# Attention weights scaled while they are turned: a product with a scaled diagonal in place of a scaled tile and a transpose

## The reference

```python
p_s = masked_softmax(einsum('btghd,btgnd->btghn', qg, ks), kpos <= q_pos)
o_s = einsum('btghn,btgnd->btghd', p_s, vs)
p_w = masked_softmax(einsum('btghd,blgd->btghl', qg, k_win), valid_w)
o_w = einsum('btghl,blgd->btghd', p_w, v_win)
out = g[..., 0:1] * o_c + g[..., 1:2] * o_s + g[..., 2:3] * o_w
```

## Time and profile before

| | us |
|---|---|
| median of three runs | 2237.94 (2236.41 to 2238.18) |
| profiled execution, its own time | 2232.05 |
| its span | 2230.2 |
| PE busy | 2080.6 (93%) |
| DVE busy | 760.7 (34%) |
| ACT busy | 470.9 (21%) |
| POOL busy | 406.0 (18%) |
| mean granted clock of TensorE | 0.956 |

### The profile page before, as it was taken

How to read it: one execution, slowest core, us unless ns; L and a number is a source line. 1 busy time by engine, 2 the same in 40 slices (tenths; PEclk the granted TensorE clock), 3 DMA queues, 4 the chain that set the end, 5 groups by cost and what they waited for, 6 DMA issues and landing times.

```text
span 2230.2 us, 28141 instructions
## 1 busy us (share of the span) xinstructions
PE 2080.6 (93%) x11199; PEld 1603.7 (72%) x11199; DVE 760.7 (34%) x1445; ACT 470.9 (21%) x869; POOL 406.0 (18%) x454
## 2 busy tenths in 40 slices
PE   4999999988878889999999998889999999899997
PEld 2555677765555556666676666789999999888875
DVE  3111233476575664311201125421111111144344
ACT  3000000134343342101100114321111111123232
POOL 0000011223232232220000035300000000045553
PEclk9999999988797889999999998999999999999999
DMA  9342001013000003543224423321112121134452
GB/s 362 109 142 95 19 20 38 1 50 110 1 1 1 1 1 111 158 115 105 75 81 113 114 99 140 130 57 43 52 38 57 38 57 38 58 139 161 152 181 104
DMA packets 179147, 188.01 MB, mean 84 GB/s; under 512 B 9957, under 2 KB 149325, under 8 KB 178574
## 3 DMA queue, kind: packets, MB, share of 16 engines
q1 hardware_dynamic: 179022, 186.26, 26.4%
HBM read 173.89 MB, written 16.53 MB: 85 GB/s over the span
## 4 chain that ended last, share of the span: by engine, by line
PE 85%; DVE 6%; DMA 3%; POOL 2%; issue 2%; ACT 1%; SPq 1%; DVEq 0%; ACTq 0%; POOLq 0%
PE ps L2375 23%; PE ps L2285 16%; PE ps L1936 13%; PE ps L2341 4%; PE ps L2343 4%; PE ps L2342 4%; PE ps L2151 3%; PE ps L2173 3%; PE ps L2134 2%; POOL arena L879 2%; DMA arena<-in_w_ada 1%; DVE arena L513 1%; PE ps L2331 1%; DMA arena<-in_w_out 1%; PE ps L1884 1%
## 5 line engine op out<-in xcount | busy, mean ns | idle before, releaser
L2375 PE MATMUL ps<-h_hi,wup_hi 128*128 128x344 f32 x1056 | 339.6, 322 | 10.6 <-issue 5.7
L2375 PE MATMUL ps<-h_lo,wup_hi 128*128 128x344 f32 x1056 | 340.2, 322 | 0.0
L2375 PE MATMUL ps<-h_hi,wup_lo 128*128 128x344 f32 x1056 | 339.9, 322 | 0.0
L1936 PE MATMUL ps<-arena,hT 128*128 128x386 f32 (+2 forms) x1152 | 320.8, 434 | 5.7 <-DVEq L1288 4.8
L1936 PEld LDWEIGHTS ps<-arena,hT 128*128 128x128 f32 x1152 | 215.0, 190 | 101.3 <-issue 16.0
L910 POOL CAST ra_hi<-arena 128x384 fp32r<-128x384 f32 (+1 forms) x90 | 51.8, 576 | 915.4 <-DVE arena L1828 488.7
L2341 PE MATMUL ps<-rw_hi,ra_hi 128*128 128x512 f32 x480 | 194.9, 406 | 18.9 <-DVE rw_lo L1682 12.6
L2285 PE MATMUL ps<-hT,arena 128*128 128x344 f32 x704 | 210.2, 457 | 0.0
L2375 PEld LDWEIGHTS ps<-h_hi,wup_hi 128*128 128x128 f32 x1056 | 200.4, 190 | 11.1 <-issue 11.1
L2375 PEld LDWEIGHTS ps<-h_lo,wup_hi 128*128 128x128 f32 x1056 | 200.2, 190 | 0.0
L2375 PEld LDWEIGHTS ps<-h_hi,wup_lo 128*128 128x128 f32 x1056 | 199.9, 189 | 0.0
(11 more groups left out here) (402 smaller groups left out, 2408.8 us busy)
## 6 DMA issues: line engine op xcount, KB each, us to landing
hT<-in_w_down SPq DMA_DIRECT2D x66, 512.0 KB, 3.2
arena<-in_w_ada SPq DMA_DIRECT2D x12, 2048.0 KB, 10.3
arena<-in_w_up SPq DMA_DIRECT2D x44, 512.0 KB, 4.6
arena<-in_w_in SPq DMA_DIRECT2D x30, 512.0 KB, 5.3
arena<-in_w_out SPq DMA_DIRECT2D x24, 512.0 KB, 3.3
arena<-in_cache_cmp_kv SPq DMA_DIRECT2D x64, 128.0 KB, 2.1
arena<-in_cache_slc_kv SPq DMA_DIRECT2D x128, 64.0 KB, 1.9
arena<-in_w_in SPq DMA_DIRECT2D x4, 1544.0 KB, 11.9
```

The costliest lines, as they stand in the source:

```text
L1936: ins = nc.tensor.matmul(ps[:, bank, 0:width], hT[:, k, n * P:(n + 1) * P], w[:, k, 0:width], start=(k == 0), stop=(k == KD - 1))
L2375: ins = nc.tensor.matmul(ps[:, bank, 0:TG], w[:, k0 + k, :], h[:, k, toks], start=(k == 0 and j == 0), stop=(k == KD - 1 and j == 2))
```

## The change

POOL no longer scales the weights. It makes one 128x128 diagonal for each item, `scaleD`, as the identity times the reciprocal and the gate of each partition, whatever `nb` is. Three buffers of it lie in space that is free at this time. PE turns each tile of the unscaled `pbuf` by an ordinary f32 product with this diagonal as moving operand: column q of the result is row q of the tile times its factor. The instruction `transpose` with the unscaled identity becomes `matmul`. The waits and their semaphores, the order of each queue, the groups, the banks and the copies stay as they were. The compressed keys' tiles (L2148) are still transposed.

```diff
@@ buffers @@
         ptbuf = [Pm[:, 5 + u, 0:SEQ] for u in range(3)]
+
+        scaleD = [room(37984 + u * P, P) for u in range(3)]
@@ POOL @@
                 pool.wait_ge(s_rec, u + 1)
-                nc.gpsimd.tensor_scalar(pbuf[u % 3][:, 0:nb * P], pbuf[u % 3][:, 0:nb * P], rec[:, u % 4:u % 4 + 1],
+                nc.gpsimd.tensor_scalar(scaleD[u % 3], ident, rec[:, u % 4:u % 4 + 1],
                                         gts[:, i, col:col + 1], ALU.mult, ALU.mult).then_inc(s_scaled, 1)
@@ PE, att_T @@
-                            ins = nc.tensor.transpose(ps[:, 4 + b, x * P:(x + 1) * P], pbuf[unit_at(t) % 3][:, o * P:(o + 1) * P], ident)
+                            u = unit_at(t) % 3
+                            ins = nc.tensor.matmul(ps[:, 4 + b, x * P:(x + 1) * P], pbuf[u][:, o * P:(o + 1) * P], scaleD[u],
+                                                   start=True, stop=True)
```

## The result

The changed kernel takes 2252.61 us (median of 4 runs, 2248.16 to 2261.01) against 2237.18 us of before: a ratio of 1.0079 with a 95% interval of 1.0055 to 1.0104. By these ratios it is slower by 18 to 21 us (the medians themselves differ by 15.4 and 19.9). The forecast was slower by 35, 2273 us: right in sign and inside its range, but nearly twice too large.

What follows compares the result with a forecast made beforehand. It took a chain of waits through TensorE (93% busy) and GpSimd's scaling as the bound. Rounds at 2.4 GHz 27, at 1.2 GHz 16, passages 4, less 12 from the clock: +35 on the median, 2273 us (0.62), range 2250 to 2290.

Steps and rivals of the forecast that it cites:

- The chain and its links: Attention rounds: transposes, copy, reciprocal, GpSimd's scaling, transposes, scores and PV in series; 5.3 us before, 5.9 after with five tiles.
- late rounds: Rounds k=8 to 15 at 2.4 GHz: about +0.66 us each, 5.3 us for a pair of heads.
- The waits for GpSimd: TensorE's transposes waiting for GpSimd's scaling in the attention: to shrink from 45 us to under 25.
- e=1's products in rounds k=0 to 7: At L2151, on the chain: 0.05 + 0.11 us per tile ahead of DVE's copy, at most four, at 2.4 GHz.
- e=0's share: At L2151, on the chain: 0.05 + 0.11 us per tile added at 2.4 GHz, GpSimd giving back 0.107 per tile beyond the first.
- the passages: From one pair of heads to the next: about 1.3 us beyond the 0.5 counted, three times, 4 us.
- The clock: Attention's early rounds: doubled instructions bring 2.4 GHz back two rounds sooner in each pair, 12 us returned.
- A: Attention: real products hold the clock at 2.4 GHz throughout; +13, 2251 us; chance 0.15.
- B: Attention: the change moves no clock, so nothing is returned; +47, 2285 us; chance 0.12.
- C: L2151: the product goes as fast as the transpose, leaving only GpSimd's 21 us gain; 2217 us; chance 0.03.
- D: L2151: the products' weight loads aren't hidden, 0.31 us more per tile; +169, 2407 us; chance 0.04.
- E: Attention: TensorE's added work fits into its 45.3 us of waits, GpSimd's return pays the rest; no change; chance 0.04.

Runs made afterwards that it cites:

- GpSimd's half alone: Kernel before with GpSimd making the 128x128 diagonal, TensorE still transposing with the identity, weights left unscaled: 2217.95 us, ratio 0.9911.
- With the clock held: Whole change on the kernel before plus idle transposes in early rounds (2223.11 us without the change): 2248.36 us; also run with only early, middle or late rounds changed.
- TensorE's half alone: Kernel before with GpSimd still scaling the weights in place, TensorE turning them by a product with the unscaled identity: 2269.98 us, ratio 1.0141.
- the second profile: Changed kernel run again unaltered, for its spread and another profile: 2255.44 us in 6 runs, ratio 1.0092.
- the idle products: Kernel before plus 3, 3 and 2 unread products ahead of TensorE's wait for scaled weights in rounds k=0, 1, 2: 2224.92 us, ratio 0.9938.
- Idle f32 transposes: Kernel before with 6, 6 and 4 unread transposes ahead of TensorE's wait for scaled weights in rounds k=0, 1, 2: 2223.11 us, ratio 0.9937.

## Why the prediction was wrong, point by point

*The chain and its links: right.* TensorE's product takes two records at a step of 0.11, 1.10 us for four tiles and 1.38 for five; GpSimd 447 ns; a five-tile round 5.95 us, forecast 5.9; late rounds +0.67, forecast +0.66. The 28 late rounds gave 18.9 us. The waits for GpSimd fell to 13.4 us, forecast under 25. GpSimd's half alone gave 20 us, forecast 21, though its profile shows 10.9 in the attention; beside the products its late rounds give the forecast 13.3.

*The step that failed: e=1's products in rounds k=0 to 7.* The prediction has "on the chain come 0.05 + 0.11 q for e=0, 0.05 + 0.11 x (the tiles ahead of DVE's copy, at most four) for e=1", and takes "0.5 each" for k=5 to 7 and 0.16 to 0.44 for the early ones at 2.4 GHz. With the clock held they gained 0.12 to 0.29, mostly 0.17. That is e=0's share alone: 0.05 + 0.11 q - 0.107 (q-1) = 0.16 for every q (only k=6, with 0.29, is well above it). With TensorE's half alone, where GpSimd gives nothing back, k=5 to 7 gained 0.40, 0.50 and 0.50 us: again e=0's share, 0.38 for three tiles and 0.49 for four, with nothing for e=1. The timeline of the kernel before shows why, in the round k=5 of the fourth pair, a place I had not looked at:

```profile
799.14 0.55 PE L2151 MATMUL ps<-const,arena 128*128 128x128 f32 x3 [0.57 <-POOL arena L879]
799.62 0.70 PE L2134 MATMUL ps<-arena 64*128 64x256 f32 x4
...
800.37 0.30 DVE L1511 TENSOR_TENSOR ps<-ps,const 128x128 f32<-128x128 f32 x1
...
800.70 0.69 DVE L1517 TENSOR_REDUCE arena<-ps 128x1 f32<-128x512 f32 x1
801.42 0.55 PE L2151 MATMUL ps<-const,arena 128*128 128x128 f32 x3
...
801.43 0.69 ACT L1037 ACTIVATE arena<-ps,arena 128x512 f32<-128x512 f32 x1 [1.05 <-DVE arena L1517]
...
802.24 0.16 DVE L1537 RECIPROCAL arena<-arena 128x1 f32<-128x1 f32 x1 [0.85 <-ACT arena L1037]
...
802.50 0.77 POOL L879 TENSOR_SCALAR arena<-arena 128x512 f32<-128x512 f32 x1 [1.33 <-DVE arena L1537]
```

There the reciprocal waits for the exponential, not for DVE's copy as in the earlier trace rows. The exponential waits for the maximum, which waits for the scores behind e=0's transposes (799.14). The e=1 transposes (801.42) run beside the exponential, and ScalarE copies them out (802.11). So the link from one e=0 to the next is transposes, scores, maximum, exponential, and e=1's are not in it. I read one late round and priced the others from it. In numbers: middle rounds 2.6 us in place of 6; early rounds at 2.4 GHz 3.1 in place of 7. At 1.2 GHz the first pair of both kernels shows the price (22.8 less 19.6 us, so 3.2, with k=4 partly at 2.4 GHz in both), so 13 for four pairs in place of 16. With 18.9 for the late rounds and 3.6 to 4.0 for the passages, against 5.5, the price at the clock of before is about 38, in place of 47.

*The clock: right in size, but not by the way that was forecast.* Had the other three pairs paid 3.2 us each in the early rounds, they would have grown by 9.6; they shrank by 2.2. So the clock returned 12 us there, the number forecast, and about 2 more in the middle rounds (k=5 and k=6 of the third pair had been at 1.2 GHz, 5.05 and 5.35 us against 4.07 and 4.31 elsewhere). 38 - 14 = 24, the attention's growth in the profiles (22 to 26). But the prediction had the clock return two rounds sooner in each pair, at k=2 or 3, by the doubled instructions of the early rounds. In the first pair nothing came back, and the low stretches that the second and third have, or in the second profile the third and fourth, still end in k=4 or k=5. What came back was the rounds k=0 of three pairs (17.2 us before, 12.2 changed), which goes with the products of the late rounds (above), and in each profile one pair without a low early round. That this makes 12 us is luck.

*What is open.* The ratios give 18 to 21 us, the attention in the profiles 22 to 26. Part of this is which runs were profiled: both of the kernel before (2232.05 and 2231.64 us) lie 3 to 6 us under the medians of their series, the first of the changed kernel (2261.01) 8 us above its own. The rest of the span, behind the attention, took between 1370.5 and 1380.4 us in the profiles of this case, with 59 to 80 us of it at 1.2 GHz, whatever the kernel; both kernels also spread over 13 to 15 us by their clock. Where a median run of the kernel before has these 3 to 6 us was not measured. Of the distance between the forecast 35 and the measured 18 to 21, the smaller price explains 9 us and the larger return of the clock 2; the last 3 to 6 us stay open.

*The rivals.* A (the clock stays at 2.4): its 2251 is nearer to the measured 2252.61 than the forecast, but by luck: the attention still had 79 and 84 us at 1.2 GHz. With idle work the clock does stay up, and then the price was 28, not A's 35. B (the clock changes nothing): excluded, by the idle products' 14 us. C and D: excluded by the step of 0.11. E: the late rounds' price did not fit into the waits. Of the signs, the four pairs grew by some 6 us each and not 8 to 10, and the low stretches did not end at k=2 or 3.

## What to carry to other kernels

A chain is priced by the link that is last in each kind of round: look at one round of every size before multiplying, since a link that holds with five tiles need not hold with three. On a stretch where TensorE's granted clock goes up and down, added TensorE work can have a return, and idle work in front of a wait can be a gain of its own, here 14 us. An f32 product with a 128-column moving tile costs two steps where a transpose costs one, so folding a scaling into a transpose pays only if the engine relieved saves more per tile on the chain than that step; here it was 0.107 us against 0.11.

## What the runs showed of the hardware

- Idle f32 transposes bring the clock back as products do: the stretch from 584.8 to 666.6 us ran at 1.00 with idle transposes, and the medians with either kind were 2223.1 and 2224.9 us.
- The same program runs its early rounds at 1.2 GHz in some pairs of heads and not in others (the fourth free of it in one profile, the second in the next), and its time goes with its mean clock, 13 us for 0.007 in the changed kernel.
- The clock of the first round behind a passage goes with what the late rounds before the passage did: of the ten profiles without idle work, k=0 ran wholly at 2.4 GHz in the five with products in k=8 to 15, and for 2.5 us or more at 1.2 in the five without.
- The first f32 weight load behind another kind of instruction costs 0.10 us at 2.4 GHz, the later ones are hidden: 1.38 us for ten instructions is about 0.27 + 0.10 + 9 x 0.11, with 0.27 us for one alone.
